# Gate and up products of the second feed-forward stage, 128 rows at a time, as seven half-size block products with the down products between them

## The reference

```python
D_FF = 2816
def swiglu(h, w_in, w_out):
    gu = h @ w_in                       # 1024 x 1024 times 1024 x 5632
    gate, up = jnp.split(gu, 2, axis=-1)
    return (jax.nn.silu(gate) * up) @ w_out     # 1024 x 2816 times 2816 x 1024
h = rmsnorm(x, norm_ffn[1]) * (1 + sc2) + sh2
x = x + g2 * swiglu(h, ffn_w_in[1], ffn_w_out[1])
```

## Time and profile before

| | us |
|---|---|
| median of 3 runs | 2914.72 (2914.66 to 2916.86) |
| the profiled execution | 2914.67 |
| its span, first to last instruction | 2913.1 |
| PE busy | 2793.5 (96%) |
| DVE busy | 1380.4 (47%) |
| ACT busy | 772.1 (27%) |
| share of PE in the chain that ended last | 89% |

### The profile page before, as it was taken

How to read it: one execution, slowest core, us unless ns; L and a number is a source line. 1 busy time by engine, 2 the same in 40 slices (tenths; PEclk the granted TensorE clock), 3 DMA queues, 4 the chain that set the end, 5 groups by cost and what they waited for, 6 DMA issues and landing times.

```text
span 2913.1 us, 32488 instructions
## 1 busy us (share of the span) xinstructions
PE 2793.5 (96%) x13274; PEld 2210.0 (76%) x13274; DVE 1380.4 (47%) x2379; ACT 772.1 (27%) x1226; POOL 270.9 (9%) x425
## 2 busy tenths in 40 slices
PE   6999798999999999999998999999999998999798
PEld 5666487888888888766765778888888887879767
DVE  6777645333334444656557613333322364431643
ACT  6454513111111111444443321111111141101132
POOL 2110000000000002000000000000000039910000
PEclk9999899999999999999998999999999998979899
DMA  5223222222222221100010111111111131112212
GB/s 218 94 80 137 74 87 72 82 92 86 72 72 86 72 74 63 73 30 22 30 71 24 37 58 51 51 43 58 43 43 58 43 95 37 44 38 45 80 35 74
DMA packets 118886, 192.52 MB, mean 66 GB/s; under 512 B 4832, under 2 KB 90048, under 8 KB 118496
## 3 DMA queue, kind: packets, MB, share of 16 engines
q1 hardware_dynamic: 106304, 147.44, 14.9%
q0 software_dynamic: 12480, 43.68, 4.9%
HBM read 177.33 MB, written 12.58 MB: 65 GB/s over the span
## 4 chain that ended last, share of the span: by engine, by line
PE 89%; DVE 7%; ACT 2%; issue 1%; DMA 0%; SPq 0%; DVEq 0%; ACTq 0%
PE psum L957 62%; PE psum L1004 5%; PE psum L1006 4%; PE psum L1005 4%; PE psum L1060 3%; PE psum L1088 3%; PE psum L1072 2%; PE psum L945 1%; PE psum L1228 1%; PE psum L1284 1%; PE psum L1345 1%; DVE arena L1850 1%; DVE arena L2120 1%; DVE arena L1732 1%; PE psum L1299 1%
## 5 line engine op out<-in xcount | busy, mean ns | idle before, releaser
L957 PE MATMUL psum<-hT_high,w_low 128*128 128x512 f32 x2304 | 679.2, 391 | 2.1 <-DVE arena L2139 2.1
L957 PEld LDWEIGHTS psum<-hT_high,w_low 128*128 128x128 f32 x2304 | 435.0, 189 | 93.7 <-DVE arena L2139 2.3
L957 PE MATMUL psum<-hT_high,w_high 128*128 128x512 f32 x1408 | 436.0, 391 | 16.0 <-DVE w_low L1944 11.9
L957 PE MATMUL psum<-h_low,w_high 128*128 128x512 f32 x1408 | 434.7, 390 | 0.0
L1952 DVE TENSOR_TENSOR arena<-arena,psum 128x1024 f32<-128x1024 f32 x44 | 53.7, 1222 | 634.5 <-PE psum L957 634.5
L957 PEld LDWEIGHTS psum<-hT_high,w_high 128*128 128x128 f32 x1408 | 264.8, 188 | 73.1 <-DVE w_low L1944 12.7
L957 PEld LDWEIGHTS psum<-h_low,w_high 128*128 128x128 f32 x1408 | 265.4, 189 | 55.4
L1962 DVE SCALAR_TENSOR_TENSOR xT<-psum,mod,xT 128x1024 f32<-128x1024 f32 x176 | 222.4, 1282 | 154.0 <-PE psum L957 154.0
L957 PE MATMUL psum<-hid_high,w_low 128*128 128x512 f32 x960 | 291.8, 390 | 1.0 <-DVE hid_low L2054 1.0
L1516 ACT ACTIVATE w_high<-wpair 128x2048 fp32r<-128x2048 f32 x62 | 118.9, 1918 | 506.6 <-DMA wpair<-in_ffn_w_out_dram 336.9
L957 PE MATMUL psum<-hid_low,w_high 128*128 128x512 f32 x704 | 216.8, 389 | 0.0
(11 more groups left out here) (278 smaller groups left out, 3338.9 us busy)
## 6 DMA issues: line engine op xcount, KB each, us to landing
wpair<-in_ffn_w_in_dram SPq DMA_DIRECT2D x44, 1024.0 KB, 5.1
arena<-in_ada_tiles_dram POOLq DMA_DIRECT2D x48, 512.0 KB, 3.6
wpair<-in_ffn_w_out_dram SPq DMA_DIRECT2D x22, 1024.0 KB, 4.8
wpair<-in_ada_tiles_dram POOLq DMA_DIRECT2D x16, 1024.0 KB, 5.3
wpair<-in_w_in_dram SPq DMA_DIRECT2D x24, 512.0 KB, 3.8
wpair<-in_b_tiles_dram SPq DMA_DIRECT2D x18, 512.0 KB, 3.3
arena<-in_ada_tiles_dram SPq DMA_DIRECT2D x8, 1024.0 KB, 16.4
out_dram<-xT SPq DMA_DIRECT2D x16, 512.0 KB, 2.7
```

Source lines behind the costliest of these rows:

```text
L957: mm = nc.tensor.matmul(dst[:, HALF * t:HALF * t + HALF], w(k), src(k)[:, HALF * t:HALF * t + HALF], start=first and n == 0 and w is high ...
```

## The change

Only the second feed-forward stage (l = 1) changes; the first keeps `ffn(0)`. The stage now runs over 22 tiles ("steps") of 128 hidden rows. The weights of a step are a 2x2 block matrix: A11 and A12 are the gate's halves over channel chunks 0 to 3 and 4 to 7, A21 and A22 the up's, each 128x512. The tokens are two halves of 512, so h is a 2x2 block matrix too. Step 0 is made in the ordinary way. Steps 1 to 21 use a seven-product scheme in place of eight block products: the operands A11, A12, A22, S3 = A11-A21, S2 = A22-S3, S4 = A12-S2, S1 = A21+A22 are each multiplied with one block of h or one of four blocks T1 to T4 that are made once, by sums of blocks of h. A product is 12 matmuls (four chunks times three parts) into one PSUM bank. P6 and P5 are accumulated onto P1 in its bank; ACT copies out P1, P7, P3 and P6 (`keep`), DVE makes four sums (X0, X1 of the gate, Y0, Y1 of the up), and then gate times up.

Between the products PE issues the down tiles of the step before: P1, down 0, P2, down 1, P7, down 2, P3, down 3, P6, down 4, P5, down 5, P4, down 6, down 7, each down tile being 6 matmuls over a single chunk of 128 hidden rows. Two accumulators take turns for them. Weights are loaded in pieces of 256 KB: four blocks of `ffn_w_in` (512 contiguous bytes each row) and two halves of the `ffn_w_out` rows a step. Every block and every split part has a single place, except the hidden rows. `t4_parts` is a new place. Waits of the stages around it (loads of the convolution weights, the stores of `xT`, GpSimd's SSM loads, the first two convolution products) now ask for the new stage's counters.

The diff, cut to its core:

```diff
+STEPS = FF // P
+PRODUCTS = ("P1", "P2", "P7", "P3", "P6", "P5", "P4")
+OPERANDS = ("A11", "A12", "S3", "S4", "S2", "S1", "A22")
+HIGH_TURN = ("A11", "A12", "S3", "S2", "S4", "S1", "A22")
...
+            def load_steps(l, f):
...
+                def step(s, first=False, last=False):
+                    if not last:
+                        if not first:
+                            sp.wait_ge(combined, combined_number(f, s, "S1"))
+                            part("A21", s + 1)
+                    if not first:
+                        sp.wait_ge(down_done, 8 * s + (176 * f - 8))
+                        down(1, s - 1)
+                    if not last:
+                        sp.wait_ge(product_done, product_number(f, s, "P1"))
+                        part("A11", s + 1)
+                        sp.wait_ge(product_done, product_number(f, s, "P2"))
+                        part("A12", s + 1)
+                        if first:
+                            sp.wait_ge(combined, combined_number(f, s, "S1"))
+                            part("A21", s + 1)
+                        sp.wait_ge(part_split, operand_number(f, s, OPERANDS, "A22"))
+                        part("A22", s + 1)
+                    sp.wait_ge(down_done, 8 * s + (176 * f - 4))
+                    down(0, s)
...
+            def feed(l, f):
...
+                def product(s, name, operand, dst, high_of, low_of, start=True):
+                    pe.wait_ge(part_split, operand_number(f, s, OPERANDS, operand))
+                    high, low = by_chunk(part_high[operand]), by_chunk(part_low[operand])
+                    for k in range(4):
+                        nc.tensor.matmul(bank[dst], high[:, k, :], high_of(k), start=start and k == 0, stop=False, skip_group_check=not start)
+                        nc.tensor.matmul(bank[dst], high[:, k, :], low_of(k), start=False, stop=False, skip_group_check=not start)
+                        mm = nc.tensor.matmul(bank[dst], low[:, k, :], high_of(k), start=False, stop=k == 3, skip_group_check=not start)
+                    mm.then_inc(product_done, 1)
+                def with_h(s, name, operand, dst, first, half):
+                    rows = slice(HALF * half, HALF * half + HALF)
+                    product(s, name, operand, dst, lambda k: hT_high[:, first + k, rows], lambda k: h_low[:, first + k, rows])
+                def with_token(s, name, operand, dst, token, start=True):
+                    product(s, name, operand, dst, lambda k: token_high[token][:, k, :], lambda k: token_low[token][:, k, :], start)
+                def down(s, b, ms, first=False):
+                    for m in ms:
+                        h = m // 4
+                        if m == 0:
+                            pe.wait_ge(hid_parts, s + (STEPS * f + 1))
+                        if m % 4 == 0:
+                            pe.wait_ge(down_split, 2 * s + (2 * STEPS * f + 1 + h))
+                        if not first or m > 1:
+                            pe.wait_ge(down_added, 8 * s + (176 * f + m - 1))
+                        cols = slice(P * (m % 4), P * (m % 4) + P)
+                        high, low = down_high[h][:, cols], down_low[h][:, cols]
+                        for n, (w, src) in enumerate(((high, hid_high_at[b]), (low, hid_high_at[b]), (high, hid_low_at[b]))):
+                            for t in range(2):
+                                mm = nc.tensor.matmul(acc[m % 2][:, HALF * t:HALF * t + HALF], w, src[:, t, :], start=n == 0, stop=n == 2)
+                        mm.then_inc(down_done, 1)
+                def step(s, b, first=False):
+                    if not first:
+                        pe.wait_ge(product_added, added_number(f, s - 1, "X1"))
+                    with_h(s, "P1", "A11", "a", 0, 0)
+                    down(s - 1, b, [0], first)
+                    with_h(s, "P2", "A12", "b", 4, 0)
+                    down(s - 1, b, [1], first)
+                    if first:
+                        pe.wait_ge(token_split, 4 * f + 1)
+                    else:
+                        pe.wait_ge(product_added, added_number(f, s - 1, "Y0"))
+                    with_token(s, "P7", "S3", "e", "T3")
+                    down(s - 1, b, [2], first)
+                    with_h(s, "P3", "S4", "c", 4, 1)
+                    down(s - 1, b, [3], first)
+                    pe.wait_ge(product_kept, kept_number(f, s, "P1"))
+                    if first:
+                        pe.wait_ge(token_split, 4 * f + 2)
+                    with_token(s, "P6", "S2", "a", "T2", False)
+                    down(s - 1, b, [4], first)
+                    pe.wait_ge(product_kept, kept_number(f, s, "P6"))
+                    if first:
+                        pe.wait_ge(token_split, 4 * f + 3)
+                    with_token(s, "P5", "S1", "a", "T1", False)
+                    down(s - 1, b, [5], first)
+                    if first:
+                        pe.wait_ge(token_split, 4 * f + 4)
+                    with_token(s, "P4", "A22", "e", "T4", False)
+                    down(s - 1, b, [6, 7], first)
+                first_step()
+                step(1, 0, first=True)
+                with pe.Fori(0, (STEPS - 4) // 2) as i:
+                    for b in range(2):
+                        step(2 * i + (2 + b), 1 - b)
+                step(STEPS - 2, 1)
+                step(STEPS - 1, 0)
+                down(STEPS - 1, 2, range(KC))
...
-                    nc.scalar.activation(hT_high[:, k, :], whole[:, k, :], ACT.Identity, bias=mod[:, l, at + k:at + k + 1]).then_inc(shifted, 1)
+                    shift = mod[:, l, at + k:at + k + 1]
+                    ins = nc.scalar.activation(hT_high[:, k, :], whole[:, k, :], ACT.Identity, bias=shift)
+                    if n == 3:
+                        if k >= 4:
+                            nc.scalar.activation(token_raw["T4"][:, k - 4, :], whole[:, k, 0:HALF], ACT.Identity, bias=shift)
+                        ins = nc.scalar.activation(token_raw["T3" if k < 4 else "T2"][:, k % 4, :], whole[:, k, HALF:S], ACT.Identity, bias=shift)
+                    ins.then_inc(shifted, 1)
...
+                def step(s, b, last=False):
+                    keep(s, "P1", gate_half[:, 0, :], bank["a"])
+                    down_highs(f, s - 1, 1)
+                    if not last:
+                        high(s + 1, "A11")
+                    gate(s, "X0")
+                    if not last:
+                        high(s + 1, "A12")
+                    keep(s, "P7", hid_raw[b][:, 1, :], bank["e"])
+                    if not last:
+                        high(s + 1, "S3")
+                    keep(s, "P3", gate_half[:, 1, :], bank["c"])
+                    keep(s, "P6", hid_raw[b][:, 0, :], bank["a"])
+                    if not last:
+                        high(s + 1, "S2")
+                        high(s + 1, "S4")
+                    down_highs(f, s, 0)
+                    gate(s, "X1")
+                    if not last:
+                        high(s + 1, "S1")
+                        high(s + 1, "A22")
+                    hidden_high(s, b)
+                high(1, "A11")
+                act.wait_ge(first_done, 2 * f + 2)
+                for t in range(2):
+                    nc.scalar.activation(gate_half[:, t, :], acc[0][:, HALF * t:HALF * t + HALF], ACT.Silu).then_inc(gate_ready, 1)
+                high(1, "A12")
+                high(1, "S3")
+                token(1, "T3")
+                hidden_high(0, 0, first=True)
+                high(1, "S2")
+                high(1, "S4")
+                token(2, "T2")
+                token(2, "T1")
+                high(1, "S1")
+                high(1, "A22", first=True)
+                token(3, "T4")
+                step(1, 1)
+                with act.Fori(0, (STEPS - 4) // 2) as i:
...
+                    if n == 3 and k < 4:
+                        dve.wait_ge(scaled, KC * (n - 1) + k + 1)
+                        nc.vector.tensor_tensor(token_raw["T1"][:, k, :], dst[:, k, HALF:S], dst[:, k, 0:HALF], ALU.subtract).then_inc(token_made, 1)
...
+                def combine(s, name, first=False):
+                    x, y, op, freeing = {"S3": ("A11", "A21", ALU.subtract, "P7"), "S2": ("A22", "S3", ALU.subtract, "P6"),
+                                         "S4": ("A12", "S2", ALU.subtract, "P3"), "S1": ("A21", "A22", ALU.add, "P5")}[name]
...
+                def add_down(s, m):
+                    dve.wait_ge(down_done, 8 * s + (176 * f + m + 1))
+                    nc.vector.scalar_tensor_tensor(xT[:, m, :], acc[m % 2], mod[:, l, 40 + m:41 + m], xT[:, m, :], ALU.mult, ALU.add).then_inc(down_added, 1)
...
+                def step(s, b, first=False, last=False):
+                    down_lows(s - 1, 1)
+                    add_down(s - 1, 0)
+                    low(s, "S4")
+                    low(s, "S2")
+                    dve.wait_ge(product_kept, kept_number(f, s, "P1"))
```

(83 more changed lines are left out.)

224 lines of the change are left out of this document (210 added, 14 removed).

## The result

The changed kernel takes 2899.74 us (median of five, 2899.05 to 2902.6), the kernel before in the same session 2915.15 us (2914.66 to 2917.11): ratio 0.9947, interval 0.9933 to 0.9962. That is 15.4 us less; 2895.6 was forecast. The execution whose profile is read here took 2902.6 us, the longest of the five; its span is 2900.7 us (before: 2914.67 and 2913.1).

The account below looks back on a forecast made before the run. PE was taken as the bound, at 0.2265 us a matmul. 46.2 + 1.4 - 13.7 - 12.1 - 2.7 = 19.1 us gained, from 2914.67 to 2895.6 us; own range 2888 to 2906, with rivals and bounds 2879 to 2918.

Parts of the forecast that it names:

- The loop: Steps of the loop: DVE's chain from P5 to the hidden low part is late, 0.7 us a step, 13.7 us lost.
- The start: norm(3) and steps 0 to 2: extra subtractions, stops and slow clock, 12.1 us lost.
- Stop (a): First down tile waits for step 0's hidden rows, behind A12's late load: 6.0 us of stop.
- Stop (b): Down 2 waits for update 0, queued behind other work on DVE and ACT: 6.6 us of stop.
- (c): Three 2048-column low parts in DVE's queue of step 1 delay P6, P5, P4 and step 2: 5.7 us.
- the clock term: At the start: slow matmuls at half clock after the long stops, 1.0 us lost.
- The last step: No next P1 covers update 7 and the hidden low part: 2.7 us lost, beside the usual 0.7.
- the tail: Last down stretch: ACT's eight turns start sooner with six matmuls a tile, 1.4 us gained; the rest as before.
- DVE keeps up (2882): Rival on the loop: DVE keeps up, the 13.7 us are not lost, 2882 us; chance 0.17.
- DVE is spaced by full durations: Rival on DVE's chain: instructions spaced by full durations, 0.8 us a step more, 2913 us, no change; chance 0.15.
- waits in DVE's queue cost 0.09 each: Rival on DVE's chain: some ten extra waits at 0.09 us, 0.9 us a step more, 2930 us; chance 0.15.

Follow-up runs that it names:

- e2: Changed kernel with DVE's low part of S3 for the next step moved behind the hidden rows' low part: 2888.39 us, 0.9907 of the kernel before.
- e4: Changed kernel with product P1 issued twice in each of 21 steps, 252 matmuls more: 2937.27 us, 1.0075 of the kernel before.
- e3: Changed kernel with both S1's sum and S3's low part moved behind the hidden low part, ACT and load order adapted: 2890.47 us, 0.9913 of the kernel before.
- e5: Changed kernel with ACT's P1 copy, the second down half's split and update 0 put earlier at the stage's start: 2895.09 us, 0.9925 of the kernel before.
- e8: Changed kernel with S3's low part and also update 7 moved behind the hidden low part: 2884.54 us, 0.9891 of the kernel before.
- e1: Changed kernel with the first convolution tile's load issued ahead of the last down half's load: 2900.5 us, 0.9946 of the kernel before.
- the repeat: The changed kernel run again without an edit, as base for the variants: 2900.18 us, 0.9945 of the kernel before.

## Why the prediction was right, and where not

The mechanism was right and its price too. The loop: 0.72 us a step forecast (the sum gives 0.51 + 0.11 + 0.10), 0.74 to 0.81 measured (0.64 or 0.71 of stop, 0.10 of restart); 13.7 us forecast for 19 steps, 14.2 measured for 18. It was ahead of the first down tile, released by the hidden low part, with DVE gapless from Y1. Moving one link out of the chain took the stop away but for 0.13 us (e2), and more cover took it away whole (e4). In the pieces the sum is less exact than in the total: it had 0.04 for the handover to PE and twice 0.05 for instructions with two waits. The trace has 0.05 for the handover where the step is written out, so that the stop there is 0.53 for the 0.51 of the sum, 0.23 where the wait stands in the loop, and of the two 0.05 at most one shows, in the 0.20 or 0.27 us from P5's end to Y1. That the sums come out alike is luck.

The start was forecast at 12.1 us and is 12.6 us (1.1 and 11.5); its single terms are further off and make up for each other. Stop (a): 5.5 us, forecast 6.0, with the clock at 0.5 for 6.8 us from 1686.9. Stop (b): 3.5 us, forecast 6.6; some 2.7 us of slow matmuls behind (a) fill the rest of it, since what ends (b) comes at DVE's time whenever PE arrives. So it held there that most of the slow matmuls lie where PE would wait for DVE anyway. (c), the later stops: 5.3 us (0.86, 0.59, 1.35 and 0.53 in step 1, 2.00 in step 2) and 0.3 of restarts, forecast 5.7. Behind step 2's stop the clock is 0.5 again for 3.4 us, eight slow matmuls of 0.2 us each, and nothing covers them: 1.6 us, where the clock term was 1.0.

The last step: 0.7 + 2.7 forecast, 3.3 measured.

The step of the prediction that failed is the tail. It said "with 6 matmuls a tile it is 1.4 us sooner. Gain 1.4 us. From there the turns and the last low part are as before." From the start of the last down stretch to the last low part it takes 32.6 us, before 31.0 (2360.15 to 2391.13): 1.6 us lost, 3.0 from the forecast. Two things were left out.

First, update 0 starts at 2347.84, 2.6 us after the stretch began, where 1.6 was forecast from the six matmuls alone. Two things keep it. The six matmuls of the first tile run behind a stop of 2.7 us and at half clock from 2345.7: the first four are drawn 1.68 us long, where behind a stop at full clock they are 1.18 to 1.21:

```profile
2345.20 1.68 PE L1375 MATMUL psum<-w_high,w_low 128*128 128x512 f32 x4 [2.51 <-DVE hid_high L2214]
```

And on DVE the low part of the last down half stands ahead of update 0. SP asks for this half only when down 7 is done, it lands 2.9 us later, and ACT's and DVE's parts of it end at 2347.0; without the half clock update 0 could have started at 2347.1, 0.7 us sooner, and not earlier. The experiments show that this is the bound: in the profiles of e2, e3, e4, e5 and e8 the first tile of this stretch ran at full clock, and update 0 still started 2.1 to 2.6 us into it, right behind that low part but for one small product of 0.16 us. DVE in order of time in e2, where the stretch begins at 2334.26:

```profile
2335.93 0.69 DVE L2209 TENSOR_TENSOR w_low<-wpair,w_low 128x512 fp32r<-128x512 f32 x1 [1.69 <-ACT w_low L1707]
2336.73 2.48 DVE L2219 SCALAR_TENSOR_TENSOR xT<-psum,mod,xT 128x1024 f32<-128x1024 f32 x2
```

Second, the copy of the first convolution tile stands ahead of ACT's first turn. The loads of the first two such tiles come late in SP's queue. SP in order of time, before and after:

```profile
2338.59 22.13 SPq L577 DMA_DIRECT2D wpair<-in_w_in_dram  x2
```

```profile
2342.72 0.33 SPq L709 DMA_DIRECT2D wpair<-in_ffn_w_out_dram  x1
2343.09 1.17 SPq L663 DMA_DIRECT2D wpair<-in_w_in_dram  x2
```

Before, the first was issued 21.6 us ahead of the last down stretch (the row puts the two loads together, the second ends it), now 2.1. And it lands late. The issues of 2340 to 2350 us in the transfers' view (KB each, median us to landing):

```profile
wpair<-in_w_in_dram SPq DMA_DIRECT2D x2, 512.0 KB, 8.8
out_dram<-xT SPq DMA_DIRECT2D x1, 512.0 KB, 6.6
```

The two landed in 7.1 and 10.5 us, where pieces of this size landed in 3.3 us in the earlier trace rows. They are in flight together, beside GpSimd's SSM loads; the store of `xT` is issued at 2349.15, only 1 us before the first tile is there. That sharing is what stretches them is likely from these rows and not tested. The forecast named store and SSM loads as moving with the stage's end and gave the move no price: it looked at each queue's order, but not at what meets there. With this load gone from the path the turn would start behind update 0, at 2349.2 and not 2351.18, 2.0 us sooner. e1 took it away and got 1.0 of the 2.0, for the reason shown there. In the five profiles with full clock the turn starts 4.6 to 5.4 us into the stretch in place of 6.0, still behind the copy of this tile, and the stretch to the last low part takes 31.2 to 32.0 us.

The rivals. That DVE keeps up (2882) is refuted by 18 stops in 18 steps. That DVE is spaced by full durations is refuted at 0.60 us from start to start for instructions of 0.68. The Trainium skill (VectorE: DVE Perf Modes, The DRAIN you can't avoid) says that the next operation does not start until the pipe is empty, and adds that one that is not held starts earlier: the trace disagrees with the first sentence and agrees with the second. The 691 ns of the Trainium skill for 512 float32 columns (same page, the section on the TRN2 errata) agrees with the durations, 683 to 690 here. That waits in DVE's queue cost 0.09 each fails on the same rows: the combination behind X1 has three waits and starts 0.60 us behind it. On matmuls the Trainium skill (TensorE: Matmul & The Clock Gate, Back-to-back issue gap) has a formula for an isolated gap at full clock, N/2.4 + 2.5 ns, by which 512 columns give an estimate of 215.8 ns; here it is 226.7, in the products and in the down tiles, and the forecast's 226.5 came from the trace.

Left open: why the stop alternates between 0.64 and 0.71 us with the two bodies of the loop. The trace shows only where it does: Y1 starts 0.20 us behind the end of P5's slot in one body and 0.27 in the other; all that follows is alike. Open as well is the handover of 0.23 us in the loop.

## What to carry to other kernels

Fewer matmuls pay their full time only as far as the other engines' chain into the next dependent product stays shorter than what covers it: write out that chain from the last product it needs, instruction by instruction with start-to-start times, and compare it with the matmuls issued meanwhile. Take the handover from a wait of the same kind, in a loop if yours stands in one: it was 0.05 us outside and 0.23 inside. If the chain is longer, first move what is not wanted at once behind its last link; then look for the second chain of nearly the same length before counting on more. At the end of a stage list what the same events release on all queues, since loads that had long landed before can become the thing waited for.

## What the runs showed that was not expected

- A busy share of PE of 100% can hide a stop in every step: 2232 and 2251 matmuls in 510 us both read as full (509.97 and 510.00), so 0.8% is seen in the count alone.
- The stop of 5.5 to 5.7 us was followed by a granted clock of 0.5 (1.2 GHz) for 6.8 us in each of eight profiles; stops of 2.0 to 3.8 us in some by 3.4 us of it, in others by none (the one that ends at 1702.4 not in the first profile of the changed kernel, its like in the repeat); stops of 0.6 to 0.7 us once every 30 us never.
- Loads land later when others are in flight: two pieces of 512 KB in 7.1 and 10.5 us beside each other and the SSM loads, where 3.3 to 4.0 us is usual in these traces, and 256 KB in 4.6 us instead of 2.9 with one more piece of 512 KB ahead.
- Behind each stop, even of 0.03 us, PE's second matmul comes 0.08 to 0.12 us late at full clock.
- DVE's last link and PE's first matmul lie 0.05 us apart where the code is written out and 0.23 us where the wait stands in PE's loop, in each of its steps (0.23 to 0.28 in e2).
- A DVE instruction of 512 float32 columns starts 0.60 us behind the one ahead, although it lasts 0.68, with one wait or with three.
- Twelve matmuls one after the other into one bank, and 24 with P1 twice, go at 0.2267 to 0.2268 us each on average: no price for staying in a bank.
